# Four modulation chunks ahead of the gate units, and ScalarE in VectorE's place for seven upper parts

## What is computed

```
sh_m, sc_m, gt_m, sh_f, sc_f, gt_f = split(silu(c) @ w_ada + b_ada, 6)      # modulation
h = rmsnorm(x) * (1 + sc_m) + sh_m
u, q, k, v, ga, gb = split(h @ w_in)                                        # w_in is 1024 x 4096
a = pool_mixer(u) @ w_pa;   o = attention(q, k, v) @ w_pb
x = x + gt_m * ((sigmoid(ga) * a + sigmoid(gb) * o) @ w_out)
h = rmsnorm(x) * (1 + sc_f) + sh_f
x = x + gt_f * moe(h)                                                       # top 4 of 32 experts
y = rmsnorm(x)
```

## Time and profile before

| | us |
|---|---|
| three runs, median (lowest, highest) | 1139.18 (1138.95, 1139.79) |
| the profiled execution, its own time | 1139.19 |
| its span, from first to last instruction | 1137.2 |
| TensorE busy | 1064.5 (94%) |
| VectorE busy | 331.8 (29%) |
| ScalarE busy | 168.8 (15%) |

### The profile page before, as it was taken

How to read it: one execution, slowest core, us unless ns; L and a number is a source line. 1 busy time by engine, 2 the same in 40 slices (tenths; PEclk the granted TensorE clock), 3 DMA queues, 4 the chain that set the end, 5 groups by cost and what they waited for, 6 DMA issues and landing times.

```text
span 1137.2 us, 14086 instructions
## 1 busy us (share of the span) xinstructions
PE 1064.5 (94%) x5882; PEld 504.6 (44%) x5882; DVE 331.8 (29%) x622; ACT 168.8 (15%) x302; POOL 66.7 (6%) x107
## 2 busy tenths in 40 slices
PE   7999899999999998989899999898989899998996
PEld 6877699843333333333333333333333333333332
DVE  4776777522121212121212111212121212121113
ACT  4453135510000000000000000000000000000001
POOL 5050000200000000000000000000000000000000
PEclk9999999999999999999999999999999999999999
DMA  9998987899999999999999999999999999999995
GB/s 308 376 259 328 384 294 311 343 418 424 429 427 428 437 427 434 430 430 433 427 433 432 431 435 428 437 428 432 433 430 436 428 413 431 435 432 424 429 426 239
DMA packets 44487, 459.36 MB, mean 404 GB/s; under 512 B 3716, under 2 KB 16072, under 8 KB 26936
## 3 DMA queue, kind: packets, MB, share of 16 engines
q1 hardware_dynamic: 42808, 455.12, 95.9%
q0 software_dynamic: 1168, 2.81, 1.0%
q10 hardware_dynamic: 464, 0.79, 0.2%
HBM read 457.12 MB, written 1.57 MB: 403 GB/s over the span
## 4 chain that ended last, share of the span: by engine, by line
DMA 48%; PE 45%; DVE 2%; SPq 2%; issue 1%; ACT 1%; POOL 1%; POOLq 0%; DVEq 0%; ACTq 0%
DMA arena<-in_w_down_dram 39%; PE ps L1801 20%; PE ps L1762 12%; DMA ring<-in_w_up_dram 4%; DMA ring<-in_w_in_dram 3%; PE ps L1790 2%; PE ps L1742 1%; DMA ring<-in_w_ada_dram 1%; DMA ring<-in_rpb_dram 1%; SPq L429 1%; PE ps L1492 1%; SPq L425 1%; PE ps L1493 1%; PE ps L1663 1%; PE ps L1494 1%
## 5 line engine op out<-in xcount | busy, mean ns | idle before, releaser
L1762 PE MATMUL ps<-ring,arena 128*64 128x512 f32 x2048 | 453.7, 594 | 5.5 <-DMA ring<-in_w_up_dram 5.4
L1801 PE MATMUL ps<-arena,x 128*64 128x512 f32 x992 | 231.9, 622 | 42.4 <-DMA arena<-in_w_down_dram 42.4
L1762 PEld LDWEIGHTS ps<-ring,arena 128*64 128x64 f32 x2048 | 142.7, 137 | 273.8 <-issue 258.6
L1801 PEld LDWEIGHTS ps<-arena,x 128*64 128x64 f32 x992 | 73.6, 143 | 199.0 <-issue 143.7
L1301 DVE TENSOR_SCALAR x<-ps 128x512 f32<-128x512 f32 x32 | 22.1, 691 | 255.2 <-PE ps L1762 255.2
L1294 DVE TENSOR_SCALAR arena<-iota,cur 128x128 f32<-128x128 f32 x64 | 19.3, 344 | 260.2 <-PE ps L1772 260.0
L1316 DVE TENSOR_TENSOR late<-ps,gtf 128x512 f32<-128x512 f32 x64 | 41.2, 686 | 180.5 <-PE ps L1801 180.5
L654 POOL COPY selbuf<-sel 96x64 bf16 (+1 forms) x32 | 24.5, 766 | 841.9 <-DVE x L1302 839.5
L1790 PE MATMUL ps<-late,arena 64*128 64x512 f32 x264 | 65.6, 615 | 1.5 <-DVE late L1316 1.5
L878 ACT ACTIVATE x<-x 128x512 f32<-128x512 f32 x32 | 20.2, 630 | 283.8 <-DVE x L1301 283.8
L1742 PE MATMUL ps<-arena 128*128 128x128 f32 x496 | 60.7, 276 | 0.0
(11 more groups left out here) (272 smaller groups left out, 862.6 us busy)
## 6 DMA issues: line engine op xcount, KB each, us to landing
ring<-in_w_up_dram SPq DMA_DIRECT2D x51, 4096.0 KB, 29.2
arena<-in_w_down_dram SPq DMA_DIRECT2D x24, 4096.0 KB, 20.5
ring<-in_w_up_dram SPq DMA_DIRECT2D x25, 2048.0 KB, 12.2
arena<-in_w_down_dram SPq DMA_DIRECT2D x13, 2048.0 KB, 18.2
ring<-in_w_ada_dram SPq DMA_DIRECT2D x16, 1024.0 KB, 10.6
ring<-in_w_ada_dram SPq DMA_DIRECT2D x16, 512.0 KB, 10.1
ring<-in_w_in_dram SPq DMA_DIRECT2D x16, 512.0 KB, 9.7
ring<-in_w_in_dram SPq DMA_DIRECT2D x8, 1024.0 KB, 8.0
```

The costliest lines, as they stand in the source:

```text
L1762: ins = mm(ps[CAP * h:CAP * h + CAP, half, :].rearrange("q (p j) -> q p j", j=4), xgT[:, place, kk, CAP * a:CAP * a + CAP], w[:, half, :, ...
L1801: ins = mm(ps[CAP * n:CAP * n + CAP, YB, :], hT[:, j, CAP * h:CAP * h + CAP], w[:, jj, n * HALF:(n + 1) * HALF], start=(jj == 0), stop=(jj ...
```

## The change

It has five parts.

1. TensorE multiplies modulation chunks 0 to 3 ahead of the gate units: one behind the pooling product, one behind the first scores, one behind the transposes of the cached keys, one behind the second scores (ADA_FIRST = 4). The other twelve stand one behind each of units 0 to 11; before, sixteen stood as 1, 1, 2 behind units 0 to 11 (ADA_AFTER).
2. For that, the product for v has PSUM banks 2 and 6 in place of 2 and 3 (V_BANK). Chunk 0 no longer waits for z_read, and the second scores, which write bank 6, now do.
3. The plan has other slots, and another order of the last two thirds of the modulation chunks against the "in" pieces.
4. ScalarE casts the upper parts of gate units 9 to 15 (gate_tops), between its sigmoids and its copies of transposed probabilities. VectorE then only subtracts for these.
5. mod_rows(1) stands ahead of split(6) and split(7) on VectorE; before, behind them.

```diff
     whole("in", 4, range(2), [10, 11])
     whole("ada", 1, range(4), [1, 2, 0, 3])
-    whole("in", 5, range(2), [1, 10])
-    whole("ada", 1, range(4, 8), [11, 2, 0, 3])
-    whole("ada", 2, range(2), [11, 2])
-    whole("in", 6, range(2), [0, 3])
-    whole("ada", 2, range(2, 6), [10, 11, 1, 2])
-    whole("in", 7, range(2), [10, 11])
-    whole("ada", 2, range(6, 8), [1, 0])
+    whole("in", 5, range(2), [1, 2])
+    whole("ada", 1, range(4, 8), [0, 3, 10, 11])
+    whole("ada", 2, range(1), [0])
+    whole("in", 6, range(2), [3, 10])
+    whole("ada", 2, range(1, 5), [11, 1, 2, 0])
+    whole("in", 7, range(2), [11, 1])
+    whole("ada", 2, range(5, 8), [2, 0, 3])
     whole("pb", 0, range(2), [2, 3])
     whole("pa", 0, range(2), [0, 1])
...
-ADA_AFTER = [1, 1, 2] * 4 + [0] * 4
+ADA_FIRST = 4
+TOP_FROM = 9
+TOPS = 16 - TOP_FROM
+ADA_AFTER = [1] * 12 + [0] * 4
...
+            def gate_tops(*units):
+
+                for n in units:
+                    act.wait_ge(unit_used, n - 1)
+                    for h in range(2):
+                        w = landed(act, "in", 4 + n // 4, h).rearrange("p (k n) -> p k n", k=4)
+                        ins = nc.scalar.activation(w_top[:, n % 2, 4 * h:4 * h + 4, :],
+                                                   w[:, :, (n % 4) * P:(n % 4 + 1) * P], ACT.Copy)
+                    ins.then_inc(w_top_ready, 1)
+
             gate_out(2, 3)
             pt_out(0)
-            gate_out(4, 5)
+            gate_tops(9, 10, 11)
+            gate_out(4)
+            gate_tops(12, 13)
+            gate_out(5)
             pt_out(1)
+            gate_tops(14, 15)
             gate_out(6, 7)
...
-                if n >= 2:
+                if n >= TOP_FROM:
+                    dve.wait_ge(w_top_ready, n - TOP_FROM + 1)
+                elif n >= 2:
                     dve.wait_ge(unit_used, n - 1)
...
-                for h in range(2):
-                    ins = V.tensor_copy(w_top[:, n % 2, 4 * h:4 * h + 4, :], w[h])
-                link(ins)
+                if n < TOP_FROM:
+                    for h in range(2):
+                        ins = V.tensor_copy(w_top[:, n % 2, 4 * h:4 * h + 4, :], w[h])
+                    link(ins)
...
+            mod_rows(1)
             split(6)
             split(7)
-            mod_rows(1)
...
-                    if k == 0:
-                        pe.wait_ge(z_read, 4)
...
-            done = [0]
+            done = [ADA_FIRST]
...
+            modulation(0)
             pe.wait_ge(bias_copied, 1)
             scores(0, kT[:, :, 0:P], 4)
+            modulation(1)
...
             ins.then_inc(kc_t, 1)
+            modulation(2)
             pe.wait_ge(row_ready, 4)
             pe.wait_ge(A_ready, 4)
+            pe.wait_ge(z_read, 4)
             scores(1, kT[:, :, P:TOK], 6)
+            modulation(3)
```

More of the change, by code:

```diff
@@ L386, in layer_kernel @@
         NT = [(n, t) for n in range(2) for t in range(2)]
+        V_BANK = (2, 6)
         AF_BANK, GT_BANK = (0, 1, 2, 3), (4, 7)
@@ L727, in z_out @@
                 for b in range(2):
-                    src = ps[:, bank + b, :]
+                    src = ps[:, V_BANK[b] if cc == 3 else bank + b, :]
                     if cc == 0:
@@ L1183, in unit_rest @@
             def unit_rest(n):
-                dve.wait_ge(w_top_ready, n + 1)
+                dve.wait_ge(w_top_ready, TOPS + n + 1)
                 w = branch_block(dve, n) if n < KB else out_block(dve, n - KB)
@@ L1475, in project_v @@
                         kk, c = 2 * q + a, slice(t * P, (t + 1) * P)
-                        mm(ps[:, 2 + t, :], hT_top[:, kk, c], early_top[:, n % 3, a, :], start=(kk == 0), stop=False)
-                        mm(ps[:, 2 + t, :], hT_rest[:, kk, c], early_top[:, n % 3, a, :], start=False, stop=False)
-                        ins = mm(ps[:, 2 + t, :], hT_top[:, kk, c], early_rest[:, n % 3, a, :],
+                        mm(ps[:, V_BANK[t], :], hT_top[:, kk, c], early_top[:, n % 3, a, :], start=(kk == 0), stop=False)
+                        mm(ps[:, V_BANK[t], :], hT_rest[:, kk, c], early_top[:, n % 3, a, :], start=False, stop=False)
+                        ins = mm(ps[:, V_BANK[t], :], hT_top[:, kk, c], early_rest[:, n % 3, a, :],
                                  start=False, stop=(kk == KB - 1))
                 ins.then_inc(early_used, 1)
-            done = [0]
+            done = [ADA_FIRST]
             def gates(*units):
```

## The result

The changed kernel takes 1150.43 us (median of 6 runs, 1149.25 to 1154.19), the kernel before on the same chip 1140.15 us (6 runs, 1138.95 to 1141.87): a ratio of 1.0093, 95% interval 1.0075 to 1.0111, slower. The forecast was 1149, with a range of 1143.0 to 1152.5. The profiled execution took 1149.44 us with a span of 1147.7, 10.5 us longer than before.

A forecast was written before the change was run, and what follows sets the result against it. The prediction took late slots before the first branch unit as the bound, with the end following one for one. Net waits 4.3, switches 0.5, late landings 1.5 and clock 3.4 made 9.7 us: 1149 us, range 1143.0 to 1152.5.

The forecast's parts named there:

- What bounds the kernel: From pooling product to first branch unit, 82.7 us: late slots, not bandwidth, bind; the expert stream fixes the rest.
- One for one: Any shift of the first branch unit's start, 161.22 us before, shifts the kernel's end by as much.
- Waits: TensorE ahead of chunks 4, 6, 8, 10 and 15: new waits of 9.8 us, old waits of 5.5 gone, net +4.3.
- late landings: Loads ending two or three of TensorE's new waits land later than the best case: +1.5 us, from 0 to +3.5.
- Switches between chunks and units: TensorE changes between chunks and gate units more often where double chunks are split: +0.5 us, an estimate.
- The clock: TensorE's clock falls to half behind the two long waits, chunks 6 and 10, 1.7 us each: +3.4 us, from 0.
- ScalarE's casts: Seven unit casts, 5.3 us, leave VectorE; TensorE doesn't see the longer chain: 0 us, at most 2 us.
- The clock stays: Rival: the new waits come but TensorE stays at 2.4 GHz, 1145.5 us; chance 0.18.
- The head start carries: Rival: chunks 6 and 10 are loaded when TensorE comes, only 1 to 2 us of waits remain, 1135.5 us; chance 0.07.
- VectorE the true bound: Rival: VectorE sets TensorE's pace at 120 to 140 us, so 5.3 us less work helps, 1143.5 us; chance 0.05.
- Late pieces at both ends: Rival: pa 1 holds the first branch unit about 1 us and chunk 4 may share DMA engines, 1152 us; chance 0.07.

The follow-up runs named there:

- e1: Changed kernel with the twelve later modulation chunks one gate unit further back (none behind unit 0); median 1137.89 us, ratio 0.9979 to the kernel before.
- e7: Changed kernel, no chunk behind units 0 and 1, two behind unit 2, then one each, new v stored behind new k; 1137.12 us, ratio 0.9974.
- e9: Changed kernel with 16, 10 and 10 unused identity matmuls ahead of chunks 4, 6 and 10; median 1148.22 us, ratio 1.0087 to the kernel before.
- e10: Changed kernel with later chunks one gate unit further back, but slots and order of the kernel before; median 1150.98 us, ratio 1.0101.
- e2: Changed kernel with VectorE casting the upper parts of all 16 gate units, ScalarE none; one run, 1153.54 us.
- e5: Kernel before with only ScalarE's casts for units 9 to 15 added; one run, 1140.74 us, the kernel before 1140.57.
- e8: Changed kernel with later chunks one gate unit further back and VectorE casting all upper parts; one run, 1142.39 us.
- e4: Changed kernel with GpSimd's store of new v moved behind its store of new k; one run, 1149.97 us.
- e6: Changed kernel with 16 and 10 unused identity matmuls ahead of chunks 4 and 6; median 1148.60 us, ratio 1.0076 to the kernel before.

## Why the prediction was right

**What bounds the kernel.** Right. The stage grew by 9.5 us and the down products, which stand on the expert stream, start 9.5 us later at first (274.35 for 264.81 us). The end came 10.5 us later in the profiled execution. The last 1 us lies in the expert stage, and I can't settle it: from the first branch unit to the end of the span takes 976.0 us before, 976.9 after, and up to 982 us in single executions of the experiments. So a stage of one execution and a median of times needn't agree to better than some us: the medians of e1 and e7 show less (2.5 and 3.5 us) than their stages (3.7 and 4.9), and those of e9 and e10 a greater loss (9.6 and 12.3 us) than theirs (6.2 and 6.8). "One for one" is shown to within that spread and no closer.

**Waits.** Forecast 1.5, 3.5, 1.0, 3.6 and 0.2 us, measured 4.56, 3.10, 0.98, 3.10 and none. Chunk 15 landed in time. The mechanism is as I put it: chunks 6 and 10 wait for slots that hang on the split of a unit multiplied shortly before. The term that was mis-sized is chunk 4's landing. I took 5.3 us for the first "in" 5 piece and 2.5 for each behind it, 89.9 us in all, and it landed at 92.92. The 5.3 came from a piece that found the queue empty and GpSimd quiet; at 79.6 us chunk 3 and GpSimd's loads were still under way, and the piece took 7.5. I had set 1.5 us aside for late landings, so 9.8 + 1.5 - 5.5 = 5.8 stands against 11.7 - 5.5 = 6.3. The holes in the DMA share came at 95.4 and 119.4 us, not at 92 and 113: they moved with chunk 4 and with the falls.

**Switches between chunks and units, 0.5 us.** The sum closes without it; 0.3 us is left for it at most.

**The clock, 3.4 us.** Two falls, 3.0 us by the rows and 3.3 by e9. The places were half wrong, chunks 4 and 6, not 6 and 10. That there were two, as in the sum, is luck in part: the wait at chunk 4, for which I had 1.5 us, grew threefold and took the fall that I had given to chunk 10. I had taken the rule of the Trainium skill ("TensorE: Matmul & The Clock Gate", section "What's actually happening"), that idleness halves the clock, to mean that each long wait costs a fall. Read so, all three long waits would have had one; the third, 3.10 us, shows 1.00. The rule tells that falls come here, the rows don't bear out that each such wait has one. The trace of the kernel before had this already, outside the two rows that I used. Of its ten waits of 2.7 to 3.6 us ahead of down products from 450 us on, eight are followed by a slow product (8.42 to 8.79 us) and two by a fast one (7.09 us), for instance:

```profile
626.79 7.09 PE L1801 MATMUL ps<-arena,x 128*64 128x512 f32 x32 [2.94 <-DMA arena<-in_w_down_dram]
655.92 8.78 PE L1801 MATMUL ps<-arena,x 128*64 128x512 f32 x32 [2.93 <-DMA arena<-in_w_down_dram]
```

**ScalarE's casts, 0 us.** Right for this kernel: in e2 the stage is 0.5 us longer without them. In e5 and e8, where TensorE waits less, they are worth 1.0 and 1.2 us. All three are single executions. A cast of a unit took 2 x 0.62 us, more than the 1.06 that I took from the earlier trace rows; that was one cast of 128x1024, these are two of 128x512.

**The rivals.** The clock stays: excluded by the two windows at 0.50. The head start carries: unit_ready 4 would have had to come before 92.7, and it came at 100.7. e1 shows that it does carry if one unit more lies between. VectorE the true bound: excluded by e2. Late pieces at both ends: half true, with chunk 4 late by 3.0 us; pa 1 was issued at 161.9, landed 5.0 us later and held nothing up (the branch unit waited 0.28 us, as in the earlier trace rows).

## What to carry to other kernels

Count, for each piece, who gives its slot back and how far ahead of its use; moving consumers forward gives nothing if the next consumer then stands closer behind its own release. Where a change of order loses, try the same order shifted by one step before giving it up: here one unit between two chunks decided between +0.9% and -0.2%. Write the stage as work plus waits plus clock falls and see that it closes, since then each experiment has one number to match.

## What the runs showed of the hardware

- Waits of 2.7 to 3.3 us on TensorE were followed by a granted clock of 0.50 in some places and by 1.00 in others. Behind 3.10 us both were seen in one execution; in e4 the clock fell behind 2.79 us and not behind 3.28; filling earlier waits moved a fall to a place that had none (e6). Behind the waits of 3.41 (e4), 4.12 (e2), 4.56 (after) and 9.90 us (e10) it fell. Each fall cost 1.5 us in the stage, but for one of 1.8 (e10) and one of 2.6 (e2). Matmuls of no use in the wait kept the clock at 1.00 and won 3.3 us of the stage (e9, one execution).
- A 1 MB load that SyncE issued with nothing else under way took 5.0 and 5.3 us (after and before), and 6.2 to 7.7 us beside GpSimd's loads and the end of an earlier piece. A store of 256 KB on GpSimd's queue cost SyncE's pieces 1.1 us at most, perhaps nothing (e4 and e7). The Trainium skill has it that queues of several engines share the same 16 DMA engines ("DMA: Bandwidth & Descriptors", section "Issuing engines are not separate DMA queues"); the longer loads agree.
